# Moving part of a sum, three low parts and some top-k rounds between the job slots of VectorE in a two-layer trunk kernel

## The reference

```
h = rms_norm(x, norm_g)
proj = h @ w_in        # columns: u, va, za | q, k, v, zb | iq, ik, iw | ga, gb
# branch A: layer_norm(gelu(va)), a masked 128-token mix per group, times gelu(u) and silu(za)
# branch B: indexer score = sum over 8 heads of iw * relu(iq . ik), top 128 admissible keys per query,
#           softmax attention over those keys, times silu(zb)
merged = sigmoid(ga + b0) * (y_a @ w_oa) + sigmoid(gb + b1) * (y_b @ w_ob)
x = x + merged @ w_out
```

## Time and profile before

| what | value |
|---|---|
| median of 3 runs | 784.16 us (783.88 to 784.85) |
| the profiled execution's own time | 784.24 us |
| its span (first to last instruction) | 782.4 us |
| TensorE busy | 765.6 us, 98% |
| weight loads of TensorE busy | 667.4 us, 85% |
| VectorE busy | 620.5 us, 79% |
| ScalarE busy | 460.9 us, 59% |
| GpSimd busy | 131.5 us, 17% |
| granted TensorE clock | 1.0 in every slice |
| DMA | 123.10 MB, mean 157 GB/s |

### The profile page before, as it was taken

The page is one execution under the profiler, slowest core; times in us unless marked ns, Lnnn a source line. Parts: engine busy times, 40 slices in busy tenths (PEclk is TensorE's granted clock), DMA queues, the critical chain, the costliest instruction groups (busy, mean ns, idle before and its releaser), DMA issues.

```text
span 782.4 us, 12238 instructions
## 1 busy us (share of the span) xinstructions
PE 765.6 (98%) x4364; PEld 667.4 (85%) x4364; DVE 620.5 (79%) x1051; ACT 460.9 (59%) x866; POOL 131.5 (17%) x125
## 2 busy tenths in 40 slices
PE   8999999999999999999999999999999999999998
PEld 7988877888899889988899788778888998999886
DVE  5767997989888874589986679888989878646895
ACT  6587875441567656834665977563335774677242
POOL 1443121000030103012214421200011201110130
PEclk9999999999999999999999999999999999999999
DMA  9847659533595548486874756783247943665784
GB/s 334 276 95 175 162 82 229 178 96 77 147 183 150 137 88 146 135 264 131 186 243 149 175 108 163 145 244 122 78 82 196 183 163 54 133 119 183 213 144 126
DMA packets 57900, 123.10 MB, mean 157 GB/s; under 512 B 3824, under 2 KB 8112, under 8 KB 57840
## 3 DMA queue, kind: packets, MB, share of 16 engines
q0 software_dynamic: 23568, 50.42, 34.6%
q1 hardware_dynamic: 33984, 71.31, 28.1%
q10 hardware_dynamic: 288, 0.59, 0.2%
HBM read 107.63 MB, written 10.49 MB: 151 GB/s over the span
## 4 chain that ended last, share of the span: by engine, by line
PE 70%; DVE 14%; issue 5%; ACT 5%; DMA 5%; SPq 0%; DVEq 0%; POOL 0%; ACTq 0%; POOLq 0%
PE bank L950 10%; PE bank L952 10%; PE bank L951 10%; PE bank L1019 6%; PE bank L1021 6%; PE bank L1020 6%; PE bank L1103 5%; DVE w_lo L1618 2%; PE bank L924 2%; DMA w_raw<-in_w_in 2%; PE bank L942 2%; PE bank L987 2%; DVE score L1687 2%; PE bank L988 2%; PE bank L989 2%
## 5 line engine op out<-in xcount | busy, mean ns | idle before, releaser
L1618 DVE TENSOR_TENSOR w_lo<-w_raw,w_hi 128x1024 fp32r<-128x1024 f32 x168 | 202.9, 1220 | 35.2 <-ACT w_hi L1190 31.0
L1190 ACT ACTIVATE w_hi<-w_raw 128x1024 fp32r<-128x1024 f32 x168 | 172.9, 1052 | 39.3 <-DMA w_raw<-in_w_out 17.9
L783 POOL DMA_DIRECT2D w_raw<-in_w_in x48 | 57.5, 1203 | 406.8 <-DVE w_lo L1618 382.5
L1019 PE MATMUL bank<-h_hi,w_lo 128*128 128x256 f32 x256 | 76.1, 297 | 2.3 <-DVEq L1819 1.3
L950 PE MATMUL bank<-h_lo,w_hi 128*128 128x512 f32 x192 | 75.4, 393 | 0.0
L952 PE MATMUL bank<-h_hi,w_hi 128*128 128x512 f32 x192 | 74.8, 389 | 0.0
L951 PE MATMUL bank<-h_hi,w_lo 128*128 128x512 f32 x192 | 74.7, 389 | 0.0
L1021 PE MATMUL bank<-h_hi,w_hi 128*128 128x256 f32 x256 | 72.4, 283 | 0.0
L1020 PE MATMUL bank<-h_lo,w_hi 128*128 128x256 f32 x256 | 72.4, 283 | 0.0
L1019 PE MATMUL bank<-hs,w_lo 128*128 128x256 f32 x192 | 56.5, 294 | 0.0
L1698 DVE MAX8 top<-score 128x8 f32<-128x256 f32 (+2 forms) x96 | 53.5, 557 | 2.9 <-DVE g_a L1861 1.0
(11 more groups left out here) (239 smaller groups left out, 1961.8 us busy)
## 6 DMA issues: line engine op xcount, KB each, us to landing
w_raw<-in_w_in SPq DMA_DIRECT2D x84, 512.0 KB, 4.6
w_raw<-in_w_in POOLq DMA_DIRECT2D x48, 512.0 KB, 6.1
w_raw<-in_w_out POOLq DMA_DIRECT2D x16, 512.0 KB, 6.8
w_raw<-in_w_out SPq DMA_DIRECT2D x12, 512.0 KB, 4.0
out<-x_sb POOLq DMA_DIRECT2D x4, 1024.0 KB, 5.8
w_raw<-in_w_oa SPq DMA_DIRECT2D x8, 512.0 KB, 3.5
w_raw<-in_w_ob SPq DMA_DIRECT2D x8, 512.0 KB, 4.2
x_sb<-out POOLq DMA_DIRECT2D x2, 2048.0 KB, 11.0
```

The source lines that it names most:

```text
L783: pool.dma_start(w_raw[:, slot], block_weights(layer, u), accum_op=ALU.add) \
L1019: nc.tensor.matmul(dst, w_lo[:, wk, col], a_hi[:, k], start=first and i == 0, stop=False, skip_group_check=True)
L1190: nc.scalar.activation(hi, w_raw[:, raw_slot(layer, u)], ACT.Copy).then_inc(s_whi.sem, 1)
L1618: nc.vector.tensor_tensor(lo, w_raw[:, raw_slot(layer, u)], hi.bitcast(F32), ALU.subtract) \
```

## The change

The raw s4 is made in two steps: its own block a22 high + a22 low in job 7, and + s3 in job 10. The last-sum slot of job 13 goes. On VectorE, weight unit 4 of group v moves from job 12 to job 13, unit 11 from job 20 to job 21, and the low part of the h sum s3 from job 18 to job 17. Top-k rounds: block 1 gains one in each of jobs 20, 21 and 27 and leaves job 29; block 2 gains two in job 29, one in 30 and one in 36, and loses two in job 37 and one each in jobs 38 and 39; block 3 loses one in job 36 and one in 41, and gains one in 37 and one in 57. Jobs 38, 39 and 41 (first gate) have none any more. Nothing is added or removed in number: s4 still takes two additions, each block 16 rounds.

```diff
-V_UNITS = dict(scalar=[0, 0, 2, 2, 4, 5, 7, 8, 10, 11], vector=[0, 1, 2, 4, 5, 6, 7, 8, 10, 11])
+V_UNITS = dict(scalar=[0, 0, 2, 2, 4, 5, 7, 8, 10, 11], vector=[1, 1, 2, 4, 5, 6, 7, 9, 10, 11])
...
-H_SUM_AT = {JOB_Q[0]: ["s5"], JOB_Q[1]: ["s3", "s6"]}
-H_LAST_SUM = JOB_V[1]
+H_SUM_AT = {JOB_Q[0]: ["s5"], JOB_Q[1]: ["s3", "s6"], JOB_Q[2]: ["s4"]}
+H_BLOCK_AT = JOB_K[3]
...
-H_LO_AFTER = {JOB_Q[2]: "s5", JOB_V[3]: "s6", JOB_V[4]: "s4", JOB_V[6]: "s3"}
+H_LO_AFTER = {JOB_Q[2]: "s5", JOB_V[3]: "s6", JOB_V[4]: "s4", JOB_V[5]: "s3"}
...
-TOPK_SLOTS = {19: [(1, 1)], 20: [(1, 1)], 26: [(1, 4)], 27: [(1, 4)], 28: [(1, 3)], 29: [(1, 3), (2, 1)],
-              30: [(2, 2)], **{n: [(2, 2)] for n in range(31, 34)}, 34: [(2, 1)], 35: [(2, 1)], 36: [(2, 1), (3, 1)], 37: [(2, 2)],
-              38: [(2, 1)], 39: [(2, 1)], 40: [(3, 1)], 41: [(3, 1)], 45: [(3, 2)], 51: [(3, 1)], 53: [(3, 2)], 55: [(3, 1)],
-              **{n: [(3, 1)] for n in (42, 44, 46, 52, 54, 56, 58)}}
+TOPK_SLOTS = {19: [(1, 1)], 20: [(1, 2)], 21: [(1, 1)], 26: [(1, 4)], 27: [(1, 5)], 28: [(1, 3)], 29: [(2, 3)], 30: [(2, 3)],
+              **{n: [(2, 2)] for n in range(31, 34)}, 34: [(2, 1)], 35: [(2, 1)], 36: [(2, 2)], 37: [(3, 1)],
+              45: [(3, 2)], 51: [(3, 1)], 53: [(3, 2)], 55: [(3, 1)], 57: [(3, 1)],
+              **{n: [(3, 1)] for n in (40, 42, 44, 46, 52, 54, 56, 58)}}
...
             def h_sum(layer, name):
 
                 a22_hi, a22_lo = (bottom(h, slice(HALF_K, KD)).bitcast(F32) for h in (h_hi, h_lo))
+                if name == "a22":
+                    dve.wait_ge(s_job.sem, s_job.at(layer, JOB_IQ[-1] + 1))
+                    vec.link(dve, nc.vector.tensor_tensor(h_sum_raw("s4"), a22_hi, a22_lo, ALU.add))
+                    return
                 s, s3 = h_sum_raw(name), h_sum_raw("s3")
                 if name == "s4":
-                    dve.wait_ge(s_job.sem, s_job.at(layer, JOB_IQ[-1] + 1))
-                    vec.link(dve, nc.vector.tensor_tensor(s, a22_hi, s3, ALU.add))
-                    vec.link(dve, nc.vector.tensor_tensor(s, s, a22_lo, ALU.add))
+                    vec.link(dve, nc.vector.tensor_tensor(s, s, s3, ALU.add))
...
+                    if n == H_BLOCK_AT:
+                        h_sum(layer, "a22")
                     for name in H_SUM_AT.get(n, []):
                         h_sum(layer, name)
...
-                    if n == H_LAST_SUM:
-                        h_sum(layer, "s4")
```

## The result

The changed kernel takes 773.35 us (median of 4 runs, 772.99 to 773.52) against 784.5 us (783.88 to 785.07) for the kernel before on the same chip: ratio 0.9857, 95% interval 0.984 to 0.9875.

A forecast was written before the change was run, and what follows sets the result against it. TensorE (98% busy) was taken as bound, losing only ten waits for VectorE (9.0 us). Terms 2 x 0.9 + 1.84 + 1.8 + 3.4 = 8.8, less 0.6, gave 8.2: from 784.16 to 776.0 us, range 774.4 to 780.2.

The forecast's parts named there:

- Job 22: Group v: the addition for job 20 no longer stands behind unit 11's low part; 1.84 us won, 1.8 in the second layer.
- Job 16: Group v: unit 6 starts 0.9 us earlier without the s4 additions in job 13; 0.9 us won a layer.
- Jobs 39 and 42: First gate: fewer rounds end both waits; 0.74 and 0.72 us won in the first layer, 0.74 and 0.35 in the second.
- rival (c): GpSimd's in-order queue: unit 8's later DMA holds up units 9 to 11, kernel slower, 787 us; chance 0.05.
- 9.0 us are to be had: Both layers: TensorE's ten printed waits for VectorE, 7.2 us, plus 0.16 to 0.25 refill each, are all that can be won.
- the low end: Range's fast end, 774.4 us: all ten waits gone (9.0), the wait for job 11's rotation too, no new one.
- the wait of `rotated(11)`: Job 12: TensorE's small wait (0.32 us) for this rotation, at 98.56, stays as it is; 0 won.
- 0.2 us a layer lost: Job 24: unit 13 takes 11.5 us to land, its low part comes just when asked for; bounds 0 and 1.0.
- keeps 0.1 of its wait: Job 43, first gate: 0.1 us of its wait stays; 0.43 us won in each layer.
- two steps ahead: Job 10: ScalarE's relus and index additions queue behind the moved addition too, but have two steps of lead.
- my bound of 0.4: Job 10: upper bound in us a layer for the new wait at the rotation's transposes, taken as 0.1, lower bound 0.
- The addition's price: VectorE: linked addition 1.30 us, 1.37 with gap, against 1.14 unlinked; by the skill's rule each moved addition costs 0.2 less.

The follow-up runs named there:

- experiment 5: The kernel before with only the low part of unit 11 moved from job 20 to job 21: 781.35 us, ratio 0.9956.
- experiment 2: The kernel before with only the changed top-k rounds: 784.16 us (780.84 to 788.46 in 10 runs), ratio 0.999.
- experiment 6: The kernel before with the changed top-k rounds and the low part of unit 11 in job 21: 776.73 us, ratio 0.9889.
- experiment 1: The changed kernel with the top-k rounds of the kernel before: 778.11 us, ratio 0.991.
- experiment 8: The kernel before with only the rounds of jobs 38, 39 and 41 moved, to jobs 43, 47 and 57: 785.37 us, ratio 1.0005.
- Experiment 9: The changed kernel with the third sum (s4 plus s3) in job 12 instead of job 10, run twice: 772.89 and 773.33 us, ratios 0.9845 and 0.9849.
- experiment 3: The kernel before with only the s4 additions moved to jobs 7 and 10: 784.54 us, ratio 0.9998.
- experiment 4: The kernel before with only three low parts moved (unit 4 to job 13, unit 11 to job 21, s3 to job 17): 780.14 us, ratio 0.9941.
- experiment 7: The changed kernel with only the low part of unit 4 put back in job 12: 776.43 us, ratio 0.9892.

## Why the prediction came out too small

**Right.** The direction, the place and the mechanism of every wait that went. Job 22: addition ahead of unit 11's low part, 3.64 forecast, 3.62 measured; experiment 5 shows it alone. Job 16: 0.9 a layer by the s4 additions leaving job 13, with ScalarE's high part last; measured 0.87 in layer 1 and, with job 17, 1.15 in layer 2. Jobs 39 and 42: 2.55 forecast, 2.49 measured. Less the start's 0.45, job 26 of layer 1 begins 2.84 us earlier (2.6 forecast) and job 44 4.90 (4.5 forecast). Job 7: nothing lost (no shift up to job 11). GpSimd's queue: units 8 and 9 were issued together and landed in 5.6 and 7.8 us (the first row below gives their median), so rival (c) had no ground. Unit 11 was issued at 115.94 and landed in 8.1, at 124.04; less the start's 0.45 that is the 123.6 of the forecast. The DMA view's rows of both issues (count, size, us to landing):

```profile
w_raw<-in_w_in POOLq DMA_DIRECT2D x2, 512.0 KB, 6.7
```

```profile
w_raw<-in_w_in POOLq DMA_DIRECT2D x1, 512.0 KB, 8.1
```

**The step that failed** is in the first section: "With 0.16 to 0.25 more for each of the ten waits, 9.0 us are to be had." From it the low end was made, "all ten waits gone (9.0), the wait of `rotated(11)` too, and no new one", 9.8 us. It took the wait view as a full list of what could be won. (The view lists a little more for VectorE, 1.8 us at L1103 and 0.6 and 0.5 at L879; of these the change could reach only the 0.6, which is `rotated(11)`.) Three more waits a layer, two for the softmax (seen at jobs 45 and 49) and one of job 50 for VectorE's addition of job 48 (seen at jobs 50 and 51), held TensorE by 0.1 to 0.3 us, too short to print, and the rounds that left the gate freed them: 1.08 us in both layers. They go in the changed kernel and in experiments 2 and 6, and not in experiment 1; experiment 8 frees the first two and makes the third longer. And the ten waits themselves were worth 9.6 us, not 9.0, though 0.2 is left at job 16 of layer 1: the forecast added only what the first matmul behind a wait loses beyond its printed idle time, while the second comes late too (next point). So 10.7 us were to be had where the low end rests on 9.0; the new wait and the wait of `rotated(11)` cancel each other.

**Terms that were mis-sized**, in order of size:

- "0.2 us a layer lost" for unit 13, with job 23 at nothing: measured 0.13 won in each layer, a difference of 0.66 in both. Unit 13, issued at 120.45, landed in 10.1 us, not 11.5, so its low part (131.69) was early enough. And the refill is longer than the one pitch that I counted: after the wait of before the second matmul of job 22 came 0.34 behind the first, where 0.23 is usual. That 0.11 is won at job 23. Of before, behind the row of 128.61:

```profile
128.95 0.40 PE L1049 MATMUL bank<-w_hi,hs 128*128 128x512 f32 x1
```

- Job 43 "keeps 0.1 of its wait": it kept none. Won 0.61 a layer, not 0.43: 0.51 at its own first matmul, and 0.10 that is the refill behind job 42's wait.
- Jobs 16 and 17: 2.01 against 1.8. In layer 1 the size was right (0.87), and 0.2 of the wait stays, where about 0.1 was forecast; in layer 2 TensorE finds the bank free, and the rest of the wait and its refill go too (1.15).
- Jobs 10 to 14: the sum was nearly right, 0.03 lost for 0.2, but by two errors. "ScalarE's relus and index additions queue behind it too; they are two steps ahead" was wrong in what it meant: two steps is all that the two buffers give, and the relu waited 0.55. The wait before job 13 is 0.46, above my bound of 0.4. Against that the sentence that `rotated(11)` "stays where it is and so does the small wait for it" was half right: VectorE's rotation is where it was (98.97 less 0.45 is 98.52, forecast 98.56), but TensorE, held up before job 13, comes 0.55 later and no longer waits for it. One lateness of VectorE is paid once, not at both places. Experiment 9 shows that it need not be paid at either, though 0.6 of the 1.1 us won there comes back at jobs 16 and 17.

Together: 1.08 + 0.66 + 0.30 (0.36 at job 43 less 0.06 at 39 and 42) + 0.21 + 0.17 + 0.14 of starts, less 0.02 at job 22, make 2.54, the difference between 8.24 (the sum before rounding) and the 10.8 between the two profiles. The medians are 11.2 apart; that 0.4 lies between executions and no trace explains it.

**What carries what.** The sums alone are worth nothing (experiment 3), the rounds alone nothing by their median (2, though its one trace, the fastest of ten executions, gains 3), the low parts 4.5 (4), yet all together 11.2. Each of the first two clears a wait and grows another that only a moved low part removes: unit 4 for the sums (7), unit 11 for the rounds (6).

**The addition's price.** The Trainium skill (VectorE: DVE Perf Modes, § The DRAIN you can't avoid) has a semaphore between two Vector instructions at no extra cost. Here the third sum of experiment 9 keeps VectorE 1.36 us (100.07 to 101.43) and a low part without a link 1.14 to 1.15 (107.47 to 108.62 in the changed kernel), both with 1.22 to 1.23 of duration. Half of the difference is not the link: behind a sum stands one more semaphore step of VectorE's own, and the two linked additions of before, which have none between them, are 1.26 apart (the second is at 106.56):

```profile
105.30 1.22 DVE L1770 TENSOR_TENSOR v_a<-h_hi,h_raw 128x1024 f32<-128x1024 f32 x1
```

That still leaves 0.11 to 0.12 for the link, so the trace does not bear the rule out for this pair, and the time of the kernel does not hang on it. (The prediction's 1.30 us of duration is half of a row of two instructions, 1.37 + 1.23; its sum uses the 1.37.)

## What to carry to other kernels

The idle times that a wait view prints are no ceiling: where the matmuls ahead are modelled as longer than their pitch, short pauses vanish, so compare the pitch of a group's first matmul and of its second with the usual one. On an in-order engine, put a piece of work that waits for a transfer behind whatever another engine is asking for; and price moves together, since one that only shifts a lateness is worth something only with the move that makes room where it lands. With a ring of two buffers, "two steps ahead" is no slack.

## What was not expected of the hardware

From 118 to 131 us VectorE's busy time rose from 8.75 to 12.04 of 13 us, and TensorE had no pause left:

```profile
118.00:131.00 13.00, 13.00 (x58) 10.56 (x57) 12.04 (x22) 7.22 (x9) 2.38 (x2) 1.00 1.08 259
```

With the same full DMA share of 1.08 as the earlier trace rows, the last of the three units landed in 10.1 us instead of 11.5. The low part of s3, now ahead of unit 9, delays unit 9's low part and with it the issue of unit 13, so the three are issued at 115.94, 118.25 and 120.45 rather than two of them together. GpSimd's timeline and the landing of unit 13 (DMA issues), first of experiment 5, where s3 has not moved, then of the changed kernel:

```profile
118.90 2.41 POOL L783 DMA_DIRECT2D w_raw<-in_w_in  x2 [1.11 <-DVE w_lo L1618]
...
w_raw<-in_w_in POOLq DMA_DIRECT2D x1, 512.0 KB, 11.6
```

```profile
120.45 1.20 POOL L783 DMA_DIRECT2D w_raw<-in_w_in  x1 [1.02 <-DVE w_lo L1618]
...
w_raw<-in_w_in POOLq DMA_DIRECT2D x1, 512.0 KB, 10.1
```

The profiles agree, in both layers: 11.5 to 11.6 us where the two are issued 1.1 us apart (the kernel before, experiments 2, 3, 5, 6 and 8), 9.7 to 10.2 where they are 2.2 or more apart (the changed kernel, experiments 1, 4, 7 and 9). Counted from the same job, unit 13 is issued 1.1 us later and lands 0.3 us earlier, and experiments 5 and 6 pay 0.20 to 0.29 a layer at job 25 that the changed kernel does not. That the transfers crowd each other less is the likely reason; no run moves the low part of s3 alone. And the stretch before job 4 was between 0.14 us shorter and 0.58 longer than in the profile of before, in experiment 7 even 3.00 longer, while the distances between jobs inside the layers repeated to 0.1 but for single places (1.6 us at job 23 of layer 2 in the second profile of the kernel before): a median of four runs can hide a shift that those distances show.
